# Index queries with 384 moving columns, compressed probabilities turned four heads at once, and six sparse steps alone instead of eight

## What is computed

```python
# compressed branch: 31 compressed keys and values for each of 2 kv heads
s = jnp.einsum('bhgtd,bhcd->bhgtc', q, kc) * scale
valid = cend[None, :] <= jnp.arange(T)[:, None]
p = jax.nn.softmax(jnp.where(valid, s, NEG_BIG), axis=-1)
o = jnp.einsum('bhgtc,bhcd->bhgtd', jnp.where(valid, p, 0.0), vc)
...
# indexer of the second block: each token keeps its 128 best keys
dots = jnp.einsum("bthd,bsd->bths", iq_b, ik)
score = jnp.einsum("bth,bths->bts", iw_b, jax.nn.relu(dots))
_, idx = lax.top_k(jnp.where(causal, score, -jnp.inf), 128)
```

## Time and profile before

| | |
|---|---|
| median of 3 runs (lowest to highest) | 1060.7 us (1060.67 to 1061.99) |
| span of the profiled execution | 1059.3 us |
| PE busy | 1049.7 us, 99% of the span |
| DVE, ACT, POOL busy | 48%, 42%, 38% |
| granted PE clock, mean | 0.999 |

### The profile page before, as it was taken

The page is one execution under the profiler, slowest core; times in us unless marked ns, Lnnn a source line. Parts: engine busy times, 40 slices in busy tenths (PEclk is TensorE's granted clock), DMA queues, the critical chain, the costliest instruction groups (busy, mean ns, idle before and its releaser), DMA issues.

```text
span 1059.3 us, 14455 instructions
## 1 busy us (share of the span) xinstructions
PE 1049.7 (99%) x5545; PEld 844.1 (80%) x5545; DVE 509.0 (48%) x1061; ACT 448.8 (42%) x788; POOL 400.2 (38%) x300
## 2 busy tenths in 40 slices
PE   9999999999999999999999999999999999999997
PEld 8877897767678876888777888888888888888886
DVE  6766788875752316998587344230000000032444
ACT  6444457676653425233465414342221221233533
POOL 3455520001025333446000255434435354465772
PEclk9999999999999999999999999999999999999999
DMA  9541141201032331332221232223232323323221
GB/s 298 184 120 51 34 119 41 75 17 44 28 120 80 72 117 43 101 99 80 80 80 41 80 104 95 91 77 110 80 118 79 114 84 104 114 80 100 82 97 80
DMA packets 84724, 95.72 MB, mean 90 GB/s; under 512 B 8121, under 2 KB 70930, under 8 KB 84666
## 3 DMA queue, kind: packets, MB, share of 16 engines
q1 hardware_dynamic: 83706, 92.46, 28.0%
q0 software_dynamic: 560, 2.12, 0.6%
q10 hardware_dynamic: 400, 0.35, 0.1%
HBM read 92.80 MB, written 2.12 MB: 90 GB/s over the span
## 4 chain that ended last, share of the span: by engine, by line
PE 94%; DVE 4%; ACT 1%; issue 1%; POOL 0%; DVEq 0%; ACTq 0%; POOLq 0%
PE bank L1882 56%; PE bank L2194 23%; PE bank L1940 4%; PE bank L1971 3%; PE bank L2012 3%; PE bank L1988 1%; DVE L L1478 1%; PE bank L2169 1%; PE bank L1833 1%; PE bank L2098 1%; PE bank L2045 1%; DVE L L1524 1%; DVE pool L1483 0%; PE bank L2001 0%; PE bank L1964 0%
## 5 line engine op out<-in xcount | busy, mean ns | idle before, releaser
L1042 POOL TENSOR_TENSOR w_lo<-raw,w_hi 128x512 fp32r<-128x512 f32 (+1 forms) x190 | 267.2, 1436 | 415.7 <-ACT w_hi L1104 403.0
L1882 PE MATMUL bank<-h_hi,w_hi 128*128 128x512 f32 (+1 forms) x560 | 224.0, 400 | 0.3 <-ACT h_hi L1315 0.2
L1882 PE MATMUL bank<-h_hi,w_lo 128*128 128x512 f32 (+1 forms) x560 | 218.6, 390 | 0.0
L1882 PE MATMUL bank<-h_lo,w_hi 128*128 128x512 f32 (+1 forms) x560 | 217.8, 390 | 0.0
L1082 POOL TENSOR_TENSOR w_lo<-raw,w_hi 128x512 fp32r<-128x512 f32 x88 | 110.7, 1290 | 133.5 <-ACT w_hi L1353 67.1
L1104 ACT ACTIVATE w_hi<-raw 128x512 fp32r<-128x512 f32 (+3 forms) x94 | 111.2, 1213 | 116.1 <-PE bank L1882 113.8
L1882 PE MATMUL bank<-w_hi,h_hi 128*128 128x512 f32 (+2 forms) x397 | 145.3, 366 | 0.0
L1882 PE MATMUL bank<-w_lo,h_hi 128*128 128x512 f32 (+2 forms) x397 | 144.5, 364 | 0.0
L1882 PE MATMUL bank<-w_hi,h_lo 128*128 128x512 f32 (+2 forms) x397 | 144.5, 364 | 0.0
L2194 PE MATMUL bank<-h_hi,w_hi 128*128 128x512 f32 x352 | 137.1, 389 | 0.0
L2194 PE MATMUL bank<-h_hi,w_lo 128*128 128x512 f32 x352 | 137.0, 389 | 0.0
(11 more groups left out here) (213 smaller groups left out, 1260.3 us busy)
## 6 DMA issues: line engine op xcount, KB each, us to landing
raw<-in_w_in SPq DMA_DIRECT2D x29, 1024.0 KB, 5.3
raw<-in_w_ffn_gate SPq DMA_DIRECT2D x11, 1024.0 KB, 5.4
raw<-in_w_ffn_up SPq DMA_DIRECT2D x11, 1024.0 KB, 5.4
raw<-in_w_out SPq DMA_DIRECT2D x8, 1024.0 KB, 5.0
raw<-in_w_ffn_down SPq DMA_DIRECT2D x8, 1024.0 KB, 5.1
raw<-in_w_in SPq DMA_DIRECT2D x8, 512.0 KB, 4.6
pool<-in_cmp_w SPq DMA_DIRECT2D x4, 1024.0 KB, 9.1
raw<-in_w_ffn_down SPq DMA_DIRECT2D x4, 768.0 KB, 4.3
```

The costliest lines, as they stand in the source:

```text
L1042: nc.gpsimd.tensor_tensor(w_lo[:, u.n % 2, cols], raw[:, u.n % 2, cols], w_hi[:, u.n % 2, cols].bitcast(F32), ALU.subtract).then_inc(lo_do ...
L1882: ins = mm(bank[t.bank][0:t.m, 0:u.width if u.token else T], stationary, moving, start=first and n == 0, stop=last and n == len(products) ...
```

## The change

Three things. The index queries are computed for tokens 128 to 511 only: a unit has a first token `t0`, and matmuls, bank columns and evacuation of `iq_u` are cut to 384 columns.

The compressed probabilities are stored as token block, head, key, so that a 128-column block of `pc` holds four heads of 32 columns (the 32nd set to zero by a DVE memset in part 1). One job now serves four heads: 4 transposes of 128 x 128, one ACT copy, and two matmuls, each with 64 rows (two heads) of `vc` stationary, into two banks. `vc` becomes block-diagonal, 128 rows by 128 columns for each group, written by four ACT copies. The memset of `PT` on GpSimd and ACT's wait for it go. The sparse list has 22 jobs and 26 steps. The waits of transposes for their bank follow a table `before_in_bank`.

With 20 steps beside projections as before, 6 run alone; the splits h_hi and h_lo that stood in the last four of eight steps are put into the last two of six.

```diff
...
+IQ0 = TOPK
+assert IQ0 % P == 0
...
-    def __init__(self, name, parts, nk, width, tiles, k0=0, first=True, last=True, act=False, token=False):
+    def __init__(self, name, parts, nk, width, tiles, k0=0, first=True, last=True, act=False, token=False, t0=0):
...
-        self.k0, self.first, self.last, self.act, self.token = k0, first, last, act, token
+        self.k0, self.first, self.last, self.act, self.token, self.t0 = k0, first, last, act, token, t0
...
-                    [Tile(0, P, kind, 2 * j), Tile(P, P, kind, 2 * j + 1)])
+                    [Tile(0, P, kind, 2 * j), Tile(P, P, kind, 2 * j + 1)], t0=IQ0 if kind == "iq" else 0)
...
-        jobs["nsa"] += [Job("nsa", ((g + n, NT - 1),), compressed=True) for n in range(2)]
+        jobs["nsa"].append(Job("nsa", ((g, NT - 1),), compressed=True))
...
-            j.nt = 1 if which == "diff" else 2
+            j.nt = 1 if which == "diff" or j.compressed else 2
...
+    before_in_bank, held = {}, {}
+    for which in ("diff", "nsa", "dsa"):
+        for j in jobs[which]:
+            for c in range(j.nt):
+                if j.t + c not in alternate:
+                    if c in held:
+                        before_in_bank[j.t + c] = held[c]
+                    held[c] = j.t + c
...
-                if which != "diff" and k == dict(nsa=1, dsa=2)[which] + LAG + 1:
+                if which == "nsa" and k == LAG + 1:
+                    enter, left[2] = enter + left[2], None
+                if which == "dsa" and k == 2 + LAG + 1:
...
-        if at == 7:
+        if at == 5:
...
-            split_high("mix", at - 1)
-        if 5 <= at < 8:
-            split_low("mix", (0, 1, 3)[at - 5])
+            split_high("mix", 2 * at - 5)
+            split_high("mix", 2 * at - 4)
+            for m in ((0,), (1, 3))[at - 4]:
+                split_low("mix", m)
...
-    assert at == 8
+    assert at == 6
...
-        vc = sb("vc", [P, KVH, DH])
+        vc = sb("vc", [P, KVH, P])
...
-                        nc.gpsimd.memset(PT[:, 0:2, 3 * P:T], 0.0).then_inc(zero_done, 1)
...
-                    act_fn(iq[:, idx, :], src, ACT.Copy).then_inc(sc_evac, 1)
+                    act_fn(iq[:, idx, IQ0:T], src[:, IQ0:T], ACT.Copy).then_inc(sc_evac, 1)
...
-                    w, rows = job.width, NCMP if job.compressed else P
-                    if which == "diff" and k == LAG:
-                        sc.wait_ge(zero_done, 2)
+                    w = job.width
...
-                        act_fn(turned(t)[0:rows, 0:w], turned_bank(t, c)[0:rows, 0:w], ACT.Copy).then_inc(pt_done, 1)
+                        act_fn(turned(t)[:, 0:w], turned_bank(t, c)[:, 0:w], ACT.Copy).then_inc(pt_done, 1)
...
-                    act_fn(vc[0:NCMP, :, :].rearrange("p a b -> p (a b)"), bank[VALUE_BANK][0:NCMP, 0:2 * DH], ACT.Copy)\
-                        .then_inc(kc_squares, 1)
+                    for q in range(4):
+                        ins = act_fn(vc[32 * q:32 * q + NCMP, :, DH * (q % 2):DH * (q % 2) + DH],
+                                     bank[VALUE_BANK][0:NCMP, 0:2 * DH].rearrange("p (a b) -> p a b", a=KVH), ACT.Copy)
+                    ins.then_inc(kc_squares, 1)
...
+                    v.memset(spread(pc[:, b, NCMP:NCMP + 1], [32, 16], [1, 1]), 0.0)
...
-                            spread(pc[:, b, P * hh:P * hh + 1], [32, NT], [1, NCMP]),
+                            spread(pc[:, b, 32 * hh:32 * hh + 1], [P, NT], [1, NCMP]),
...
-                    lc = spread(pc[:, b, 0:1], [P, GROUP], [32, NT], [1, NCMP])
+                    lc = spread(pc[:, b, 0:1], [32, GROUP], [P, NT], [1, NCMP])
...
-                    chain(v.tensor_tensor(spread(csm[:, 0:1], [NT, GROUP], [1, NT]), spread(csm[:, 0:1], [NT, GROUP], [1, NT]),
+                    chain(v.tensor_tensor(spread(csm[:, 0:1], [1, GROUP], [GROUP, NT]), spread(csm[:, 0:1], [1, GROUP], [GROUP, NT]),
...
-                        moving = (h_hi, h_lo, h_hi)[p][:, h, :]
+                        moving = (h_hi, h_lo, h_hi)[p][:, h, u.t0:T]
...
-                    ins = mm(bank[t.bank][0:t.m, 0:u.width if u.token else T], stationary, moving, start=first and n == 0,
+                    out_cols = slice(0, u.width) if u.token else slice(u.t0, T)
+                    ins = mm(bank[t.bank][0:t.m, out_cols], stationary, moving, start=first and n == 0,
...
-                    if enter is not None and job.which != "diff":
-                        wait_free(pe, pt_at[max(job.t - 2, 0):job.t])
-                    elif t in turned_before:
-                        wait_free(pe, [pt_at[turned_before[t]]])
-                    elif t in alternate:
+                    if t in alternate:
...
-                    elif t >= job.nt:
-                        wait_free(pe, [pt_at[t - job.nt]])
+                    elif t in before_in_bank:
+                        wait_free(pe, [pt_at[before_in_bank[t]]])
...
-                        h = 2 * job.g + c
-                        pe.wait_ge(cmp_p_done, h // GROUP + 1)
-                        for j in range(NT):
-                            o = P * (h % GROUP) + 32 * j
-                            ins = nc.tensor.transpose(dst[0:NCMP, P * j:P * j + P], pc[:, h // GROUP, o:o + NCMP], ident)
+                        pe.wait_ge(cmp_p_done, job.g // 2 + 1)
+                        for o in range(0, T, P):
+                            ins = nc.tensor.transpose(dst[:, o:o + P], pc[:, job.g // 2, o:o + P], ident)
...
-                    O = bank[O_BANKS[job.g % 2]]
...
-                        pe.wait_ge(o_out, job.g - 1)
-                    for half in range(2):
-                        ins = mm(O[DH * half:DH * half + DH, :], vc[:, job.g // 2, :], turned(job.t + half),
+                        pe.wait_ge(o_out, job.g)
+                    for n in range(2):
+                        rows = slice(DH * n, DH * n + DH)
+                        ins = mm(bank[O_BANKS[n]][:, :], vc[rows, job.g // 2, :], turned(job.t)[rows, :],
...
-            idle_rows = vc[:, :, :].rearrange("p a b -> p (a b)")
+            idle_rows = vc[:, 0, :]
```

## The result

| | before | after |
|---|---|---|
| median of 5 runs each, us | 1060.92 | **1052.66** (1052.51 to 1053.07) |
| ratio, 95% interval | | 0.9922 (0.9910 to 0.9934) |
| span of the profiled execution, us | 1059.3 | 1051.0 |

Forecast: 1052.8, range 1049.8 to 1056.2. The time came out where it was forecast; not every step of the working did. In after the lines have moved: scores L1954 (L1940 before), projection matmuls L1896 (L1882), transposes L1979 (L1971) and, compressed, L1972 (L1964), values L2020 (L2012) and, compressed, L2009 (L2001), head transposes L2160 (L2152), logits L1536 (L1524), h_lo L1785 and, behind a norm, L1793 (L1772, L1780).

A forecast was written before the change was run, and what follows sets the result against it. PE's back-to-back matmuls were taken to bound the kernel, so PE work removed is time won. Terms -4.75 + 2.9 - 6.82 + 0.5 + 0.3 = -7.9 us, from 1060.7 to 1052.8 us; range 1049.8 to 1056.2.

The forecast's parts named there:

- Index queries: Index matmuls on 384 instead of 512 columns: 173.6 ns each, first tile giving back 0.4 us; -4.75 us.
- Beside the projections: Twenty sparse steps beside projection pieces: +1.58 us of PE work and 1.3 us of waits, +2.9 us.
- The reason for the waits: Near 208 us: ACT's four exponentials delay a tanh DVE needs, so PE waits for logits; 1.3 us.
- Steps alone: Stretch of sparse steps without projections, six instead of eight: DVE sets the pace, 22.98 to 16.16 us, -6.82 us.
- The h_lo stall: Output projection: the k = 1 split stands behind DVE's last output product, so PE waits; +0.5 us.
- Small things: Two DVE memsets in the compressed logits, +0.2 us, and a longer memset of vc, +0.1 us.
- no new waits: Rival: DVE and ACT keep up everywhere, the stretch alone falls to PE's own 14.3 us; 1049.1 us, 10%.
- bound loads: Rival: weight loads set index matmul spacing at 384 columns, 188 instead of 173.6 ns; 1054.2 us, 8%.
- values that don't overlap: Rival: the two compressed value matmuls of a job run one after the other, 2.1 us; 1054.9 us, 6%.
- a tail without its gain: Rival: DVE and ACT enter the steps alone with a backlog, half the gain there; 1056.2 us, 9%.
- steps whose time comes back as waits: Rival: the removed steps' time returns as waits in the stretch beside projections; 1059 to 1062 us, 3%.
- The slower one: Rival: DVE becomes the bound of the dense steps, costing time in 18 steps; 1065 us, 3%.

The follow-up runs named there:

- e7: The kernel after with index queries on 256 moving columns instead of 384, leaving out tokens 128 to 255: 1049.13 us.
- e5: The kernel after with sparse steps 1 and 2 each two projection pieces later, first scores at piece 5 as before: 1052.65 us.
- e9: The kernel after with DVE's four norm products of the differential heads moved behind projection pieces 9, 11, 13 and 15: 1051.80 us.
- e10: The kernel after with the four norm products behind pieces 9, 11, 13 and 15, and sparse steps 1 and 2 two pieces later: 1051.98 us.
- e4: The kernel after with transposes and gains of heads 0, 1 and 2 moved from the steps alone into the last three projection pieces: 1057.35 us.
- e11: The kernel after with one of DVE's three copies of turned probabilities in the last steps made by ScalarE: 1052.40 us.
- e3: The kernel after with h_lo[1] split ahead of the last steps and h_lo[2] behind them: 1051.82 us.
- e8: The kernel after with transposes put between scores and compressed values in one step: 1052.63 us.

## Why the prediction was right, and where not

- **Index queries, -4.75: -4.46.** The spacing was forecast at 173.6 ns and is 173.5 (72 matmuls in 12.49 us). The first tile went from 6.22 to 5.59: it gave back 0.66 of its 1.29, not 0.4. That term was too small, since DVE's 0.67 us for each h_lo piece holds nearly the whole tile; e7 shows the end of it, a first tile that gains nothing more. The second unit was put 8.7 us behind the first index matmul (48 steps of 173.6 ns and the 0.4) and started 9.76 behind it (347.75 to 357.51): the working left out that in before the first tile took 6.22 and not 24 x 0.227 = 5.45. So GpSimd's weights had more cover than forecast, and PE did not wait for them.
- **Beside the projections, +2.9: +2.33.** Waits 1.0 instead of 1.3. PE's work by difference +1.3 instead of +1.58: the compressed values took 0.95 to 0.99 instead of 1.06, and the scores ahead of them 0.94 to 0.97, about 0.2 us for each of the two jobs, because they are neighbours of one shape (0.1 us the other way is not traced). The step that failed is a price from a row with other neighbours. The transposes, 0.41 (209.62 to 210.03), were forecast at 0.43.
- **The reason for the waits.** The tanh behind the exponentials was foreseen with its place and time, and sets when the first of the three waits comes; that the other two follow I had put to one coefficient step. e5, e9 and e10 show a fuller cause: DVE's norm products and weight splits, which it does in the same pieces. That a dense stretch leaves DVE 23% free was read from 218 to 240 us, just behind this.
- **Steps alone, -6.82: -6.85.** The number was right, the reason was not. I held DVE for the clock and PE's own work for 14.3 us. That is the step that failed. By the starts in after PE's work is some 15.0 us: four head transposes 1.9, two scores 2.1, six values 6.1, five transposes 4.8; these took 0.93 to about 1.0 and not 0.85, and not only ahead of other shapes: ahead of the 128-row head transposes it was 0.93, for which no run here gives a cause. The remaining 1.1 are waits, 0.7 of them idle time in the rows. I took one wait of 0.44 us in the earlier trace rows for a sign that DVE sets the pace, and never added up PE's work in that stretch of before, which by its busy time was fuller than DVE's. Since the two are near each other, a count of either gives about the same sum, and that the number came out so close is luck. e4 tells them apart; e11 doesn't, as it loads ScalarE.
- **The h_lo stall, +0.5: +0.55**, with its place. e3 takes it away.
- **Small things, +0.3: +0.13.** DVE's two memsets, forecast at 0.2 together, last 0.07 us each (at 127.07 and 138.96 in after) and are not to be seen by the scores at 159.75 (0.0). They were taken as full cost because a wait for logits stood somewhere behind; but between them and that wait DVE sits idle for 1.98 us, until 153.49, for ScalarE's weights. The longer memset of `vc`, forecast at 0.1, does hold the warm-up matmuls (1.11 for 1.01 us), and the first projection matmul came 0.16 later. With a spread of up to 0.9 us at that place, whether the memset made this is not shown.

So the costs were over-estimated by 0.2 + 0.6 us, and the index gain by 0.3; the errors have opposite signs, and the sum of -7.9 us stands against -8.3 measured. That the time is within 0.2 us of the forecast is luck in part: the forecast starts from 1060.7 us, and the five executions of before beside the result have 1060.92. The rivals: "no new waits" fell by the rows at 208 to 218 us, bound loads by e7, values that don't overlap by their 0.95, a tail without its gain by the 16.12 us, and steps whose time comes back as waits by the +2.33. The slower one had its mechanism, DVE as the bound, right for five pieces and not for eighteen steps.

## What to carry to other kernels

Price an operation on TensorE from a row where the same shape stands ahead of it and behind it: here a border between 64-row and 128-row matmuls was worth 0.1 to 0.2 us. Before an engine is called the clock of a stretch, add up the other engines' work by rows of that stretch; where two come out within a tenth of each other, only an experiment that unloads one alone, and loads no third engine in its place, can tell. A wait that goes when its apparent cause is moved, and comes back one piece later, belongs to an engine that is full, so look at its busy share over exactly those pieces.

## What the runs showed of the hardware

Weight loads of 188 to 191 ns with matmuls 120 ns apart (e7): they overlap each other and do not set the spacing at 256 columns. The two more borders of e8 cost 0.39 us. And the start of the first projection matmul varies by up to 0.9 us between executions (12.9 to 13.8), nearly all of it in the time that the warm-up matmuls take (7.1 to 8.1 us), which is as much as most of the edits tried here are worth.
